# Dilated attention over 704 keys a tile, queries sorted by position modulo 4, rotary rows gathered

## The reference, cut to what matters

```
DILATED_PATTERNS = ((128, 1), (512, 4), (2048, 16))
for window, d in DILATED_PATTERNS:
    half = window // (2 * d)
    o, lse = banded_attention(to_strided(q, d), to_strided(k, d), to_strided(v, d), half)
    ...
w = softmax(stack(lses)); o = sum(w * outs)
```

## Time and profile before

| | |
|---|---|
| median of 3 runs | 3017.72 us (3017.17 to 3019.48) |
| profiled execution: its own time | 3021.17 us |
| its span, first to last instruction | 3019.1 us |
| mean granted PE clock | 0.997 of full |
| PE busy | 2967.6 us, 98% |
| DVE busy | 1929.9 us, 64% |
| ACT busy | 1037.9 us, 34% |
| POOL busy | 1381.3 us, 46% |
| chain that ended last, by engine | PE 81%, DVE 11%, ACT 3%, DMA 3% |

### The profile page before, as it was taken

The page is one execution under the profiler, slowest core; times in us unless marked ns, Lnnn a source line. Parts: engine busy times, 40 slices in busy tenths (PEclk is TensorE's granted clock), DMA queues, the critical chain, the costliest instruction groups (busy, mean ns, idle before and its releaser), DMA issues.

```text
span 3019.1 us, 37919 instructions
## 1 busy us (share of the span) xinstructions
PE 2967.6 (98%) x14232; PEld 2355.2 (78%) x14232; DVE 1929.9 (64%) x1852; ACT 1037.9 (34%) x1434; POOL 1381.3 (46%) x1100
## 2 busy tenths in 40 slices
PE   9999999998999999999999999999999999999998
PEld 7776668885778888888877777888678788888886
DVE  8989875435376677786566565311575767778764
ACT  3005773105143422332335353312652434223321
POOL 3334333330254677775333333333443556767760
PEclk9999999999999999999999999999999999999999
DMA  3111002130112422322131212331431233232331
GB/s 145 49 42 35 1 20 93 43 124 15 35 62 100 150 101 97 126 98 105 55 123 60 77 59 73 133 135 45 190 126 49 70 112 137 99 121 98 105 112 56
DMA packets 76626, 262.43 MB, mean 87 GB/s; under 512 B 7360, under 2 KB 8000, under 8 KB 73152
## 3 DMA queue, kind: packets, MB, share of 16 engines
q1 hardware_dynamic: 57696, 183.96, 17.9%
q10 hardware_dynamic: 18784, 76.49, 6.6%
HBM read 207.46 MB, written 52.95 MB: 86 GB/s over the span
## 4 chain that ended last, share of the span: by engine, by line
PE 81%; DVE 11%; ACT 3%; DMA 3%; issue 1%; POOL 1%; ACTq 0%; DVEq 0%; SPq 0%; POOLq 0%
PE psum L606 48%; PE psum L887 15%; PE psum L1101 3%; PE psum L938 2%; DVE cacc L1710 2%; DMA hid<-TT 2%; PE psum L738 2%; PE psum L723 2%; PE psum L986 2%; PE psum L709 2%; PE psum L853 1%; DVE SX L1958 1%; DMA raw<-weights 1%; PE psum L1052 1%; DVE WSX L1958 1%
## 5 line engine op out<-in xcount | busy, mean ns | idle before, releaser
L472 POOL TENSOR_TENSOR small<-par 128x1 f32<-128x1 f32 x168 | 44.9, 267 | 1143.8 <-PE psum L606 990.0
L606 PE MATMUL psum<-A_hi,w_hi 128*128 128x512 f32 x1536 | 481.7, 395 | 2.2 <-DVE RU L1681 0.8
L606 PE MATMUL psum<-A_lo,w_hi 128*128 128x512 f32 x1536 | 473.4, 389 | 0.0
L606 PE MATMUL psum<-A_hi,w_lo 128*128 128x512 f32 x1536 | 472.8, 389 | 0.0
L478 POOL TENSOR_TENSOR w_lo<-raw,w_hi 128x1024 fp32r<-128x1024 f32 (+1 forms) x152 | 386.1, 2540 | 12.7
L606 PEld LDWEIGHTS psum<-A_hi,w_hi 128*128 128x128 f32 x1536 | 287.2, 188 | 72.0 <-issue 12.2
L606 PEld LDWEIGHTS psum<-A_lo,w_hi 128*128 128x128 f32 x1536 | 288.3, 188 | 60.4
L606 PEld LDWEIGHTS psum<-A_hi,w_lo 128*128 128x128 f32 x1536 | 288.3, 188 | 60.3
L606 PE MATMUL psum<-B_hi,w_hi 128*128 128x512 f32 x832 | 258.0, 391 | 1.0 <-DVE B_lo L2170 1.0
L606 PE MATMUL psum<-B_hi,w_lo 128*128 128x512 f32 x832 | 256.1, 389 | 0.0
L606 PE MATMUL psum<-B_lo,w_hi 128*128 128x512 f32 x768 | 236.5, 389 | 0.0
(11 more groups left out here) (338 smaller groups left out, 5508.6 us busy)
## 6 DMA issues: line engine op xcount, KB each, us to landing
raw<-weights SPq DMA_DIRECT2D x256, 512.0 KB, 3.3
hid<-TT ACTq DMA_DIRECT2D x60, 512.0 KB, 2.7
XSF<-hid SPq DMA_DIRECT2D x48, 512.0 KB, 5.0
BM<-rel_bias ACTq DMA_DIRECT2D x8, 1152.0 KB, 7.6
gate_spill<-RU SPq DMA_DIRECT2D x16, 512.0 KB, 3.1
ULF<-hid SPq DMA_DIRECT2D x6, 1024.0 KB, 6.9
x_spill<-H ACTq DMA_DIRECT2D x1, 4096.0 KB, 11.2
R<-gate_spill ACTq DMA_DIRECT2D x8, 512.0 KB, 4.6
```

Of the source, the lines that this page charges most:

```text
L606: last = pe.matmul(PJ[s][:, c:c + step], w[:, s, k, :], b[:, k, c:c + step], start=(k == 0 and i == 0), stop=(k == kblocks - 1 and i == 2))
```

## The change

The q, k and v jobs now come as four of q, four of k, four of v (the weights are laid out so on the host; same bytes). DVE writes each q and k result sorted by class: position 4a + c goes to column 256c + a, so that it stores with a step of 1024 bytes. ACT's queue then copies the 16 rotary rows of each head from SBUF to SBUF, 32 DMAs of 8 partitions, so that x1 of all heads of q and k lies in RX[0] and x2 in RX[1]. After the first v result DVE rotates them all in six passes; 32 DMAs on ACT's queue write them back, then two masks are loaded and ACT copies V. The `rot` matrix and its products are gone. 61 taps stand among the jobs (`QKV_TAPS`); the last tap of a tile writes U itself, with one copy of a column behind it, and ACT's `store_conv` is gone.

A query tile is now a class r and a half (512 positions). It needs the 512 keys of its own half, the 128 keys of its class in the other half, and 64 keys across the border: 704 (with the border keys of its own class masked there). Scores, mask, exponential and scaling run over 704 columns. Probabilities are turned in six slots of 128 (the last padded with zeros), six a head; ACT copies slots 0 to 3 of each head, DVE slots 4 and 5 of both heads in one copy. V has ten key tiles instead of eight. The output of four pairs shares one bank of 512 columns instead of two in turn, and is put back in order of position while its halves are written. There are eight masks of 128x704; two come early, two after the write-backs, four when the last job is done.

```diff
+QKV_TAPS = (6, 6, 6, 6, 6, 6, 6, 6, 2, 6, 5)
+KEYS = CLASSES * P + P + EDGE
@@ PE @@
-            def turn(g):
...
+            def turn(m):
+                pe.wait_ge(free[m % 2], ROUNDS["qkv"] + 4 + m // 2 + 1)
+                if 0 < m < 3:
+                    pe.wait_ge(S["v_copied"], m)
+                at_col = 1024 if m == 3 else 0
+                for c in range(CLASSES):
+                    for half in range(2):
+                        to, keys = at_col + P * (2 * c + half), T[m % 2][:, HALF * half + c:HALF * half + HALF:CLASSES]
+                        last = pe.transpose(PX[:, to:to + P], keys, ident[:])
...
@@ pair_scores: p == 0 waits for S["roped"] 512 @@
-                for c in range(0, SEQ, HALF):
+                for at_key in (0, HALF, HALF + P):
                     for h in range(2):
...
+                            n, moving = HALF, keys[:, :, P * half:P * half + P]
...
+                            n, moving = P, K[rows, m, other:other + P]
...
+                            n, moving = EDGE, keys[:, :, edge:edge + 16].rearrange("p c a -> p a c")
@@ pair_turn @@
+                if p:
+                    pe.wait_ge(S["copied_t"], 2 * p - 1 + h)
+                    if h == 0:
+                        pe.wait_ge(S["copied_e"], p)
...
+                for side in range(2) if h == 0 else (1, 0):
+                    for k in range(2 if side else 4):
...
@@ pair_values @@
+                pe.wait_ge(S["copied_t"], 2 * p + 2)
+                pe.wait_ge(S["copied_e"], p + 1)
+                if p and r == 0:
+                    pe.wait_ge(S["attended"], 2 * m + half)
...
             for g in range(11):
                 job(ROUNDS["qkv"] + g // 2, g % 2, A)
-                if g:
-                    turn(g - 1)
+                if g > 8:
+                    turn(g - 9)
             job(ROUNDS["qkv"] + 5, 1, A, order=[0, 1, 2, 3])
-            turn(10)
+            turn(2)
+            job(ROUNDS["qkv"] + 5, 1, A, order=[4, 5])
             pair_scores(0)
-            job(ROUNDS["qkv"] + 5, 1, A, order=[4, 5, 6, 7])
+            job(ROUNDS["qkv"] + 5, 1, A, order=[6, 7])
...
@@ ACT @@
+            for g in range(8):
+                evacuated(ROUNDS["qkv"] + g // 2, g % 2)
+                for h in range(2):
+                    for part in range(2):
+                        at_row = 16 * g + ROT * h
+                        act.dma_start(RX[part][at_row:at_row + ROT, :], rows_of(g, h, part)).then_inc(S["gathered"], 16)
+            for part in range(2):
+                act.wait_ge(S["rope_made"], part + 1)
+                for g in range(8):
+                    for h in range(2):
+                        at_row = 16 * g + ROT * h
+                        act.dma_start(rows_of(g, h, part), RX[part][at_row:at_row + ROT, :]).then_inc(S["roped"], 16)
+            for t in (2, 3):
+                load_mask(t)
+            for m in range(3):
+                copy_v(m)
@@ DVE, the q, k, v jobs @@
+            def rope():
+                dve.wait_ge(S["gathered"], 512)
+                for part in range(2):
+                    chain(dve.tensor_tensor(RS[part][:], RX[1 - part][:], sinT[:], ALU.mult))
+                for part in range(2):
+                    chain(dve.tensor_tensor(RX[part][:], RX[part][:], cosT[:], ALU.mult))
+                    op = ALU.add if part else ALU.subtract
+                    tl["rope_made"](dve.tensor_tensor(RX[part][:], RX[part][:], RS[part][:], op))
             for g in range(11):
+                if g < 8:
+                    wait_job(dve, ROUNDS["qkv"] + g // 2, g % 2)
+                    out = (Q, K)[g // 4][:, g % 4, :].rearrange("p (c a) -> p a c", c=CLASSES)
+                    rows = lambda t: t.rearrange("p (a c) -> p a c", c=CLASSES)
+                    dve.tensor_tensor(out, rows(PJ[g % 2]), rows(rstd[:]), ALU.mult).then_inc(free[g % 2], 1)
...
+                if g == 8:
+                    rope()
+                for j in range(at_tap, at_tap + QKV_TAPS[g]):
@@ DVE, the attention's iteration i @@
                 if i < PAIRS:
                     pair_invert(i)
+                if i >= 3 and (i - 3) % 4 == 3:
+                    pair_out_lo((i - 3) // TT, (i - 3) % TT // 4)
                 if i + 1 < PAIRS:
                     pair_mask(i + 1, 0)
                     pair_mask(i + 1, 1)
-                if i >= 3 and (i - 3) % 4 == 3:
-                    pair_out_lo((i - 3) // TT, (i - 3) % TT // 4)
...
+                if 1 <= i <= PAIRS:
+                    pair_copy(i - 1)
+                for j in range(at_tap, min(at_tap + (1 if i % 3 else 2), 3 * TAPS)):
+                    tap(1 + j // TAPS, j % TAPS)
+                    at_tap = j + 1
```

More of the change, by code:

```diff
@@ new lines, in pair_turn, with pair_values @@
+                if p == 26 and h == 0:
+                    pe.wait_ge(S["ln_copied"], 1)
+                for side in range(2) if h == 0 else (1, 0):
+                    for k in range(2 if side else 4):
+                        key = HALF * side + P * k
+                        last = pe.transpose(turned_to(h, side)[:, P * k:P * k + P], P1[h][p % 3][:, key:key + P], ident[:])
+                    if not (h == 0 and side):
+                        last.then_inc(S["probs_t"], 1)
+            def pair_values(p):
+                m, t = p // TT, p % TT
+                half, r = t // CLASSES, t % CLASSES
+                pe.wait_ge(S["copied_t"], 2 * p + 2)
+                pe.wait_ge(S["copied_e"], p + 1)
+                if p and r == 0:
+                    pe.wait_ge(S["attended"], 2 * m + half)
+                tiles = [2 * c + half for c in range(CLASSES)] + [2 * r + 1 - half, 2 * CLASSES + half]
+                for k, tile in enumerate(tiles):
+                    for h in range(2):
+                        last = pe.matmul(PX[DH * h:DH * h + DH, 1024 + P * r:1024 + P * r + P],
+                                         V[:, tile, 2 * DH * m + DH * h:2 * DH * m + DH * h + DH], PT1[p % 2][:, h, k, :],
+                                         start=(k == 0), stop=(k == SLOTS - 1))
+                last.then_inc(S["pv"], 1)
@@ L1235, in _ @@
             wait_job(act, ROUNDS["qkv"] + 5, 1)
[L1236 removed]
+            for t in range(4, TT):
+                load_mask(t)
             copy_v(3)
@@ L1708, in tap @@
                 a, b = max(0, -sh), min(SEQ, SEQ - sh)
-                done = tl["conv_done"] if order == TAPS - 1 else chain
-                done(dve.scalar_tensor_tensor(cacc[:, a:b], u(a + sh, b + sh), w, cacc[:, a:b], ALU.mult, ALU.add))
+                out = u(a, b) if order == TAPS - 1 else cacc[:, a:b]
+                chain(dve.scalar_tensor_tensor(out, u(a + sh, b + sh), w, cacc[:, a:b], ALU.mult, ALU.add))
+                if order == TAPS - 1:
+                    chain(dve.tensor_copy(u(b, SEQ), cacc[:, b:SEQ]))
             chain(dve.memset(acc[:], 0.0))
```

300 lines of the change are left out of this document (135 added, 165 removed).

## The result

The changed kernel takes 3002.26 us (median of 5 runs, 3001.26 to 3004.28); on the same chip the kernel before takes 3017.72 (5 runs, 3015.66 to 3019.48). The ratio is 0.995, interval [0.9936, 0.9965]: 15.5 us faster, where 42.3 were forecast and 2960 to 2992 was the range. The profiled execution took 3001.26 us with a span of 2999.5. Against the profiled execution of before (3021.17, span 3019.1) that is 19.9 us. Medians of the experiments are compared with the changed kernel's as well, though they were taken beside other runs of the kernel before; its median there was 3017.75 to 3018.51, so such differences are good to about 1 us.

The account below looks back on a forecast made before the run. PE, busy for 98% of the span, was taken as the bound; -34.5 - 4.9 - 2.6 - 6.0 + 5.7 = -42.3 took the profiled 3021.17 us to 2978.9, or 2975.4 against the median 3017.72; range 2960 to 2992.

Parts of the forecast that it names:

- the one on ACT's queue: Before pair 1: 32 write-backs priced 0.48 us apart, then masks and V copy; path 39.2 us from DVE's first V result.
- Start of the attention: Pairs 1 to 5: 16.8 us for 21.7, 4.9 gained, with 0.5 lost waiting for masks.
- The q, k, v jobs: Jobs before the attention: PE loses rotary products, DVE gets more work; pair 1's scores at 259.8 for 254.07, 5.7 lost.
- DVE's list: DVE's own work in the q, k, v jobs: ends at 258.7, 37.3 us counted from its first V result.
- The slower rival: Write-backs on one queue hold PE and DVE: every 0.1 us per issue above 0.48 costs 3.2; 3024 at 2.0; chance 0.03.
- Results of q and k at 2.0 us: Eight DVE results stored with a step of 1024 bytes take 2.0 us each, 16.0 in all; bounds 1.2 and 2.0.
- The reading row: Profile row of DVE reading 2048 values at the 1024-byte step in 3.86 us, used to price stepped stores.
- The pitch: Attention loop, pairs 5 to 27: 4.45 us a pair for 6.02, bounds 4.3 and 4.8; 34.5 us gained.
- The dear-pitch rival: Attention loop: DVE at 4.9 us a pair or PE's small matmuls at 4.8 set the pitch; 2986; chance 0.17.
- End of the attention: From 417.06 to w_out's first matmul 30.5 us for 36.45, 6.0 gained; 2.6 more between pairs 27 and 28.
- I add 3.9: End of the attention: 3.9 us (0 to 7) on PE's 26.6, as layer-norm work no longer fits beside a pair.
- about what it has: End of the attention: cover of the 6.55 us reciprocal behind the second sum shrinks by 0.7, about what it has.

Follow-up runs that it names:

- grouped kernel: Changed kernel with the same bytes moved in 8 gathers and 8 write-backs for 32 and 32, each over 8 partitions and four blocks: 2986.45 us.
- The runs without the step: Changed kernel with attention output halves stored without a step, by stepping PE's writes to the output bank instead (2996.73 us) or leaving the step out (2997.27 us).
- the one with the step in the bank: Changed kernel with PE's value products writing the output bank with a step of 16 bytes, so both output halves need none: 2996.73 us.
- the one with V first: Changed kernel with two of ACT's three copies of V moved ahead of the write-backs, still 32 of them: 2991.05 us.
- the fastest one: Changed kernel with grouped transfers, the step in PE's output bank, and ACT's fourth layer-norm square moved behind the high half: 2978.65 us.

## Why the prediction was wrong

**The step that failed is the one on ACT's queue** in "Start of the attention" and "The q, k, v jobs". The queue was named, the V copy was put behind it, and even a rival was built on it; but its price was taken from SP's small loads at 0.48 us, and so its path came out at 39.2 us beside 37.3 for DVE's list, of which I added 1.1. Counted from DVE's first V result, as there:

- First half rotated: 5.5 forecast, 9.1 measured. Two of the four passes ahead of it took 2.10 and 3.30 us, for 1.22, beside POOL's weight split (220.9 to 226.1). The forecast charged the splits to the taps and not to the rotation, which is the one place where the delay moves the queue.
- 32 issues: 32 x 0.48 = 15.4 forecast, 21.1 measured, 0.66 each.
- From the end of the V copy to pair 1: 16.2 forecast, 18.2 measured. PE came back from 19 us of standing still to a granted clock of 0.87.

That is 3.6 + 5.7 + 2.0 = 11.3 us on the 39.2; the masks and the V copy add 0.2, so the path took 50.7. With 0.8 of the path that the forecast did not add, and DVE's first V result 2.1 earlier than its list had it (219.3 for 258.7 - 37.3 = 221.4), this is the whole miss at pair 1: 11.5 + 0.8 - 2.1 = 10.2, 270.04 for 259.8. The overlap that the forecast counted on was not there: the path lies 14.0 us above DVE's list (256.02 in the grouped kernel), not 1.9. The slower rival had the right mechanism and the wrong point: "from 0.48 us on, every 0.1 costs 3.2" gives 5.8 for 0.66, and the late rotation adds its own. The runs show it from both sides: no write-backs give pair 1 at 257.48, fewer ones 256.02, other order 259.36. DVE's list, forecast at 258.7, is itself right within 2.7.

**Results of q and k at 2.0 us: right** (1.95). The reading row was a good bound for stores. The Trainium skill (Advanced Engine Details and Errata, SBUF Cachelines) has a different 16-byte line at each access pay a penalty; the traces agree for these stores, 1.95 us with the step and 1.23 without. But taking the steps away gives only 2.9 of the 6.2 us, as DVE's taps then take 3.8 us more beside POOL's splits.

**The pitch: right where nothing disturbs it.** 4.42 us forecast as 4.4: scores 1.50, transposes 1.46, values 1.46, for 1.49, 1.44 and 1.44. The small matmuls are not held by their weight loads beyond the forecast's allowance: the 64 keys 1024 bytes apart were given the price of 128, and the scores came out at it. What is missing are the halves of the output. The forecast gave "low halves 0.2" and waits of "up to 0.1" every fourth pair, as if the step in them had no price, though the step in q and k was priced. They took 1.10 and 1.13 us. PE waited 0.43 to 1.07 us for the low half three times in these 22 pairs, and twice 0.47 and 0.82 us for masks that stand behind a low half and two taps on DVE: 22 x 4.42 = 97.3 became 101.1. The runs without the step give back 3.0 of it. The dear-pitch rival named "0.1 for strided low halves", far too little; its 2986 does not hold the result either, which lies above the whole range.

**End of the attention: 7.1 us for 8.6 forecast.** The wait at pair 28's values, 2.79 us, has the squares ahead of the high half, as the forecast said in "I add 3.9"; the stepped half comes on top of it. w_out's jobs lose 2.8 us more. The reciprocal now ends 4.1 us behind w_out's first matmul (427.14), for 1.2 before, and everything behind it comes later: PE waits 0.89 us for the last low half of the attention, and 0.15 and 0.72 for those of the convolution.

```profile
424.11 0.69 DVE L1869 COPY PT<-psum 128x512 f32<-128x512 f32 x1 [3.89 <-PE psum L750]
424.72 6.54 DVE L1917 RECIPROCAL acc<-acc 128x1024 f32<-128x1024 f32 x1
432.40 0.74 PE L627 MATMUL psum<-A_hi,w_hi 128*128 128x512 f32 x2 [0.89 <-DVE A_lo L1860]
```

The cover that I called "about what it has" shrank by 2.9, not 0.7. 2.0 us of it are DVE's new copy of the tail slots: what the reciprocal needs is ready at 422.68, but DVE stands at the copy, which waits for PE's transposes. No run moved it.

**Stages left as they are: 3.7 us lost**, where the forecast put nothing. The gain over the trace of before is 23.6 us at the weight splits around 470 and 20.0 from 2564 on; what is lost in between shows in waits of PE of 0.1 to 1 us for DVE and for POOL's splits. This is no fixed price of the change. The program of these stages is the same in all the kernels, yet between the same two points the grouped kernel and the one with the step in the bank lose 3.6 and 3.7, the one with V first 2.2, the one without write-backs 0.0, the one whose halves are stored without a step 4.6, and the fastest one 1.2. So, as far as these kernels show, it goes with the moment at which each engine reaches these stages, or with the single execution: each trace is one, and the executions of one kernel scatter by 1.2 to 3.3 us (by 6.8 without write-backs). Which of the two stays open, and there is only one trace of before to count from, whose time lies 3.45 us above its median. For the same reason differences of a microsecond or two between the medians of these kernels say little of the stage that an edit changed; the starts in the traces say it.

The miss in full, in the traces: 42.3 forecast, 19.9 measured; 10.3 at the start, 0.8 in pairs 1 to 5, 3.3 in the loop, 1.5 at its end, 2.8 in w_out and 3.7 behind it.

## What to carry to other kernels

A DMA's issue time belongs to the queue that issues it, here 0.66 us of ACT's for each. Count transfers, not bytes, on each queue, take the price from a transfer of the same kind, and look at what else that engine must do behind them: here four blocks in one transfer were worth 15.8 us, and two copies ahead of the issues 11.2. If a layout change makes some operation step through memory, price the step at every place where it appears, results and output halves alike, and try to put it where it is free; for this kernel that was what TensorE writes, and the worst place was what it reads as the moving operand. And before work is pulled forward, ask whether the engine will then only wait: here such a kernel came out 2.5 us slower, with TensorE's clock lower behind the wait.

## What was not expected of the hardware

- Issuing one transfer between two places of on-chip memory on ACT's queue takes 0.66 us at 8 partitions and 32 KB, 0.69 to 0.72 at 8 partitions x 4 blocks and 128 KB; a mask of 352 KB from off-chip memory takes 0.47 in the changed kernel.
- A step of 16 bytes costs by side. In the keys, PE's moving operand: 1175 ns for 641 over 512 keys, with the queries' step, whose weight loads take 310 for 186, in the same run. In what PE writes to PSUM: nothing (277 ns for 279). In ACT's and DVE's halves of 512 columns, stored so (DVE reads one input so too): 1.10 for 0.59 and 1.13 for 0.69 us.
- After PE had stood for 4.23 us, the clock granted over the next 4.2 us was 0.61 of full speed, for 1.00 in the grouped kernel, where PE had been at work since 236.5. There it was 0.69 from 236 to 246, behind a wait of 3.59 us. After 19 us it was 0.87 over the next 12; after 2.67 us, in the kernel with V first, it was 1.00.
- Passes of DVE that take 1.22 us alone took 2.10 and 3.30 us beside POOL's weight split.
